# A two-layer decoder trunk: the residual rows keep their place in SBUF, the expert ring goes from 22 units to 20, and the router's place table is built by another chain

## The chip, the cores and the metric

One core of a Trainium2 chip runs the whole kernel. The metric is device time in microseconds, median of the runs. The engines are TensorE (PE in the profile, PEld for its weight loads), VectorE (DVE), ScalarE (ACT), GpSimd (POOL) and SyncE (SP). SP issues nearly all loads; in the profile "SPq" is a transfer issued from SP's queue.

## The reference, cut to what matters

Two layers run over 512 rows of width 1024 in f32. Layer 0 mixes by differential attention, layer 1 by latent attention. Each is followed by a mixture of experts with 32 experts, of which each row takes two:

```python
for i in range(DEPTH):                      # 2 layers
    h = modulate(rms_norm(x, norm_mix[i]), sh_m, sc_m)
    y = diff_attention(h, ...) if i % 2 == 0 else mla_attention(h, ...)
    x = x + g_m[:, None, :] * y
    h = modulate(rms_norm(x, norm_ffn[i]), sh_f, sc_f)
    x = x + g_f[:, None, :] * hier_moe(h, ...)   # top-1 of 4 groups, then top-2 of its 8 experts
...
hid = jax.nn.silu(t @ w1) * (t @ w3) * combine   # per expert, 1024 -> 256
out = out + hid @ w2                             # 256 -> 1024
```

The last addition of each layer needs x as it stood before the experts ran. These are the residual rows.

## The kernel before, in words

**Work.** The rows stand on chip in X, four tiles (t = 0 to 3) of 128 rows. After each attention comes a stage that adds the mixer's product to X (DVE L1931, L1932), normalises it into XN, writes XN to the DRAM tensor xn_d (POOL L2506), and computes the router's logits. The router (`gate` on DVE, `route` on PE) then picks two experts for each row and makes `idx`, the list of rows that each pair of experts gathers. Experts are worked on in 16 pairs (n = 0 to 15), 64 places for each expert. For a pair POOL gathers 128 rows of XN by indirect DMA into RV (L2515). PE turns them (L969 for the first pair, L951 for the others), ACT and DVE modulate them (DVE L2142, L2124), and PE multiplies by w1 (signals "a"), by w3 ("b") (both L979), turns the hidden rows (L986) and multiplies by w2 ("y", L994; L1009 for the last pair). DVE weighs the result (L2155), and POOL scatters it to y_d (L2529), except for the last pair, which PE adds by a product (L1084). What doesn't fit into 64 places goes through an extra tile ("overflow") between pairs 8 and 9. At the layer's end y_d is read back into Y, and DVE adds it to X.

**Weights.** Each pair needs six units of 1 MB: two of w1, two of w3, two of w2, so a layer needs 96. They go through a ring of places (SLOTS = 22). Three banks of six lie in the buffers ring, RQK and AHS, two places in the buffer spare, and two (slots 18 and 19, X_SLOT) are X itself. Unit u of a layer goes to `slot_order[l][u % SLOTS]`. SP issues the units in one fixed order: the first 18 or so while the attention stage runs, each once the buffer under it is free; then it waits for the first two gathers; then it loads the two X places, and from there on unit u waits for the product that last read unit u - SLOTS:

```python
if u < SLOTS:
    free_at_first(l, slot)
else:
    before, part = divmod(u - SLOTS, 6)
    sp.wait_ge(sem("aby"[part // 2]), PAIRS * l + before + 1)
```

**The rows meanwhile.** Since weights are laid over X, POOL writes X to kept_d after each tile's norm (L2507), and SP reads it back near the layer's end: for layer 0 in `stream(1)` (L501), for layer 1 after the last experts (L636). The SP program runs layer 0 and layer 1 one after the other; the layer 0 read of Y (L521, L525) waits for the last scatter, that of layer 1 is issued by ACT (L1676).

**Identity products.** `keep_busy(bank, n)` (L741) issues n products of the identity with itself, whose result nobody reads. The profile records two of them for each product.

Of the kernel before, what the change touches and what calls it, by code (L numbers as in the profile page):

```python
# [68 lines left out]
SLOTS = BANKS * RING + 4  # L69
END_BANKS = (2, 3), (4, 7), (0, 1), (5, 6)  # L70
X_SLOT = BANKS * RING
SPARE_AT = {22: X_SLOT + 2, 38: X_SLOT + 3}
# [157 lines left out]
def build(nc, A, out):  # L230
    stack = ExitStack()
    with stack:
# [16 lines left out]
        kept_d = [nc.dram_tensor(f"kept_d{l}", [S, D], F32) for l in range(2)]  # L249
# [151 lines left out]
        half_of, place, over_cap, raw = scratch(PS, 2 * T), scratch(PS, 2 * T), scratch(PS, 2 * T), scratch(PS, 2 * T)  # L401
# [36 lines left out]
        def unit(s):  # L438

            if s < RING:  # L440
                return ring[:, s, :]
            if s >= X_SLOT + 2:
                return spare[:, s - X_SLOT - 2]
            if s >= X_SLOT:
                return X[:, 2 * (s - X_SLOT):2 * (s - X_SLOT) + 2, :].rearrange("p t n -> p (t n)")
            base = RQK if s < 2 * RING else AHS
            return base[:, s % RING * UNIT:(s % RING + 1) * UNIT]
# [6 lines left out]
        plan, arrival, fills, holder = [], [{}, {}], [0] * SLOTS, [None] * X_SLOT  # L454
# [3 lines left out]
        fills[X_SLOT:] = [1, 1, 1, 1]  # L458
        for l in range(2):
# [10 lines left out]
            slot_order.append([14, 15] + list(range(RING, 2 * RING)) + [18, 19, 20, 21] + unheld + held + [16, 17, 12, 13])  # L470
# [4 lines left out]
            if l == 0:  # L475
                fills[X_SLOT:] = [n + 3 for n in fills[X_SLOT:]]
            holder = [("y", PAIRS - 2)] * RING + [None] * (2 * RING)
        in_x_slot = len([u for u in range(6 * PAIRS) if u % SLOTS == X_SLOT])
        for t in range(T):
            own = in_x_slot  # L480
            loaded["rows", t] = 16 * (1 + own + 2)
            loaded["mla", t] = loaded["rows", t] + 16
            loaded["last rows", t] = loaded["mla", t] + 16 * (own + (2 if t else 1))
        s_w = [sem(f"w{s}") for s in range(X_SLOT)] + [sem("xl0"), sem("xl1"), sem("xl2"), sem("xl3")]
# [13 lines left out]
        def _(sp):  # L498
# [12 lines left out]
            def stream(l):  # L511
                for n, entry in enumerate(plan[l]):
                    if l == 0 and n in SPARE_AT:
                        first_units(0, SPARE_AT[n])
                    if l == 1 and n == 0:
                        sp.wait_ge(sem("y"), LAST - 2)
                        load_x(kept_d[0], 0)
# [12 lines left out]
            def free_at_first(l, slot):  # L530
# [12 lines left out]
                elif slot < X_SLOT:  # L543
                    sp.wait_ge(*((sem("omla"), 8) if l else (sem("oe"), 8)))
                elif slot >= X_SLOT + 2:
                    if l:
                        sp.wait_ge(sem("res"), T + 1 + slot - X_SLOT)
                else:
                    sp.wait_ge(sem("kept_out"), 16 * T * (l + 1))
# [38 lines left out]
            for l in range(2):  # L588
# [14 lines left out]
                else:  # L603
                    first_units(1, 4, 5, 6, 7, 8, 9, 10, 11, 16, 17, 12, 13, 20, 0, 1, 2, 3, 21, 14, 15)
# [42 lines left out]
            sp.wait_ge(sem("out"), 16 * (T + 2))  # L647
# [3 lines left out]
        def _(pe):  # L651
# [266 lines left out]
            def route(l):  # L918

                pe.wait_ge(sem("el"), 2 * (l + 1))  # L920
                keep_busy(3, 16)
                pe.wait_ge(sem("M"), l + 1)
                ranks = PB[6][:, 0:T * E].rearrange("p (t e) -> p t e", t=T)
                mm(PB[6][:, 0:T * E], trib[:, :], Mb.rearrange("p t e -> p (t e)"), start=True, stop=False)
# [14 lines left out]
                keep_busy(3, 16 if l else 22)  # L939
# [785 lines left out]
        def _(dve):  # L1725
# [226 lines left out]
            def add_at_end():  # L1952

                dve.wait_ge(sem("out"), 16)
# [33 lines left out]
            def gate(l):  # L1988
# [46 lines left out]
                tt(hot_step, oh[:, :, 0:PAIRS], oh[:, :, PAIRS:], ALU.add)  # L2035
                link(red(half_of, oh[:, :, PAIRS:], AX.X, ALU.add))
# [597 lines left out]
```

## Time and profile before

| what | us |
|---|---|
| median of 3 runs | 1110.64 |
| lowest, highest | 1109.88, 1111.30 |
| the profiled execution, its time | 1109.18 |
| the profiled execution, its span in the trace | 1107.4 |
| mean granted clock of TensorE in it | 0.988 of full |

The trace covers the span of 1107.4 us; 1.8 us of the profiled execution's time lie around it. All positions in the text are microseconds from the span's start. The stage of layer 0's experts begins near 342, that of layer 1 near 856.

### The profile page before, as it was taken

The numbers are of one execution on the slowest core, as the hardware profiler recorded it, in microseconds if no ns is written. First come the engines' busy times: TensorE is split into PE (matmuls) and PEld (weight loads), VectorE is DVE, ScalarE is ACT, GpSimd is POOL, SyncE is SP. The second block draws the span as 40 slices with busy tenths as digits, with TensorE's granted clock in tenths as the row PEclk, the third lists the DMA queues.
The fourth block names the chain that finished last, engine by engine and source line by source line (L and its number), as shares of the span: only waits on it lengthen the run. The fifth ranks groups of instructions, "written<-read, shape, count | busy, mean of one in ns | idle before, by whom it ended". The sixth has DMA issues, their size and how long they took to land.

```text
span 1107.4 us, 15314 instructions
## 1 busy us (share of the span) xinstructions
PE 1041.3 (94%) x5662; PEld 630.0 (57%) x5662; DVE 611.5 (55%) x1479; ACT 328.6 (30%) x891; POOL 92.0 (8%) x129
## 2 busy tenths in 40 slices
PE   6999999999998999898889999999998899979986
PEld 5444444555458666565556566565456666646652
DVE  6799989898647422222246577877236622222224
ACT  4321111874231211111114555666122211111110
POOL 1000000000011212121000000000000111101100
PEclk8999999999998999999999999999999999999999
DMA  9939967947578999999996400401837899999998
GB/s 366 404 132 395 393 264 297 386 171 297 235 291 328 401 419 418 418 418 419 417 394 269 166 1 1 189 2 50 367 115 305 346 419 419 417 397 417 419 416 351
DMA packets 66814, 341.44 MB, mean 308 GB/s; under 512 B 11110, under 2 KB 11366, under 8 KB 36400
## 3 DMA queue, kind: packets, MB, share of 16 engines
q1 hardware_dynamic: 49952, 297.68, 66.7%
q0 software_dynamic: 15120, 37.63, 8.9%
q10 hardware_dynamic: 1664, 5.09, 1.2%
q8 instruction: 48, 0.79, 0.3%
q14 instruction: 30, 0.25, 0.1%
HBM read 320.90 MB, written 37.24 MB: 323 GB/s over the span
## 4 chain that ended last, share of the span: by engine, by line
PE 75%; DMA 10%; DVE 5%; SPq 4%; ACT 3%; issue 3%; ACTq 0%; DVEq 0%; POOLq 0%
PE PP L979 16%; PE PP L732 12%; PE PP L842 10%; PE PP L994 8%; DMA AHS<-in_moe_w 5%; SPq L565 4%; PE PP L754 3%; PE PP L1199 3%; PE PP L1165 2%; PE PP L1203 2%; DMA AHS<-y_d 2%; PE PP L802 2%; PE PP L705 2%; PE PP L791 2%; PE PP L951 1%
## 5 line engine op out<-in xcount | busy, mean ns | idle before, releaser
L732 PE MATMUL PP<-ring,AHS 128*128 128x512 f32 x320 | 139.9, 592 | 0.0
L2148 DVE TENSOR_TENSOR PS<-PS,PP 128x256 f32<-128x256 f32 x33 | 13.9, 421 | 193.2 <-PE PP L979 183.7
L842 PE MATMUL PP<-ring,AHS 128*128 128x512 f32 x256 | 112.2, 594 | 0.0
L732 PEld LDWEIGHTS PP<-ring,AHS 128*128 128x128 f32 x320 | 59.7, 190 | 69.8 <-issue 69.8
L2155 DVE SCALAR_TENSOR_TENSOR PS<-PP,small,GF 128x512 f32<-128x512 f32 x66 | 46.5, 747 | 95.8 <-PE PP L994 85.4
L842 PEld LDWEIGHTS PP<-ring,AHS 128*128 128x128 f32 x256 | 47.8, 190 | 56.9 <-issue 56.9
L1642 ACT ACTIVATE PS<-PP 128x256 f32<-128x256 f32 x33 | 12.6, 383 | 216.5 <-PE PP L979 186.8
L979 PE MATMUL PP<-RQK,RV 128*64 128x256 f32 x640 | 71.9, 379 | 2.7 <-issue 2.7
L979 PE MATMUL PP<-AHS,RV 128*64 128x256 f32 (+1 forms) x592 | 68.7, 380 | 2.3 <-DVE RV L2142 1.3
L979 PE MATMUL PP<-ring,RV 128*64 128x256 f32 (+1 forms) x528 | 64.3, 391 | 4.1 <-issue 2.1
L979 PEld LDWEIGHTS PP<-RQK,RV 128*64 128x64 f32 x640 | 54.7, 137 | 21.9 <-issue 8.9
L979 PEld LDWEIGHTS PP<-AHS,RV 128*64 128x64 f32 (+1 forms) x592 | 51.1, 138 | 19.5 <-issue 6.6
L979 PEld LDWEIGHTS PP<-ring,RV 128*64 128x64 f32 (+1 forms) x528 | 49.1, 144 | 20.7 <-issue 8.7
L2529 POOL DMA_INDIRECT y_d<-PS,row x31 | 31.8, 1027 | 329.0 <-DVE PS L2155 286.1
L1872 DVE TENSOR_REDUCE small<-PP 128x2 f32<-128x256 f32 (+3 forms) x64 | 52.5, 822 | 8.5 <-PE PP L757 8.4
L2124 DVE TENSOR_SCALAR RV<-PP,small 128x128 f32<-128x128 f32 x124 | 42.4, 406 | 24.1 <-PE PP L951 23.2
L1748 DVE SCALAR_TENSOR_TENSOR ring<-ring,PS 128x1024 f32<-128x1024 f32 x44 | 51.8, 1221 | 4.3 <-DMA ring<-in_ada_t 3.9
L1646 ACT ACTIVATE PS<-PP 128x256 f32<-128x256 f32 x33 | 12.6, 383 | 136.4 <-PE PP L986 136.4
L1618 ACT ACTIVATE RV<-PP,small 128x128 f32<-128x128 f32 x124 | 46.6, 456 | 3.5 <-PE PP L951 3.5
L741 PE MATMUL PP<-ident 128*128 128x128 f32 x280 | 40.3, 307 | 4.4 <-POOL GM L2435 2.2
L1429 ACT ACTIVATE AHS<-PP,small 128x256 f32<-128x256 f32 (+3 forms) x82 | 41.1, 510 | 11.0 <-DVE small L1872 10.8
L1748 DVE SCALAR_TENSOR_TENSOR AHS<-AHS,PS 128x1024 f32<-128x1024 f32 x36 | 42.5, 1222 | 1.5 <-DMA AHS<-in_ada_t 1.0
(366 smaller groups left out, 1711.4 us busy)
## 6 DMA issues: line engine op xcount, KB each, us to landing
AHS<-in_moe_w SPq DMA_DIRECT2D x54, 1024.0 KB, 23.0
RQK<-in_moe_w SPq DMA_DIRECT2D x52, 1024.0 KB
ring<-in_moe_w SPq DMA_DIRECT2D x49, 1024.0 KB, 21.9
ring<-in_ada_t SPq DMA_DIRECT2D x22, 1024.0 KB, 21.1
AHS<-in_ada_t SPq DMA_DIRECT2D x18, 1024.0 KB
spare<-in_moe_w SPq DMA_DIRECT2D x16, 1024.0 KB, 13.6
X<-in_moe_w SPq DMA_DIRECT2D x16, 1024.0 KB
ring<-in_da_w_qkv SPq DMA_DIRECT2D x10, 1024.0 KB, 13.3
```

What stands on the lines that cost most here:

```text
L565: sp.dma_start(unit(slot), (w1, w3, w2)[k // 2][l][n + PAIRS * (k % 2)]).then_inc(s_w[slot], 16)
L732: last = mm(PB[qkv_bank(n)][:, :], HT[:, c, t * P:(t + 1) * P], us[c // 4][:, (c % 4) * NH:(c % 4 + 1) * NH], start=c == 0, stop=c == C - 1)
L741: mm(PB[bank][:, 0:P], ident[:, :], ident[:, :], start=True, stop=True)
L842: last = mm(PB[2 * t + n][:, :], (OT, OTM)[l][:, k, t * P:(t + 1) * P], us[k // 2][:, (k % 2) * D + n * NH:(k % 2) * D + (n + 1) * NH], st ...
L979: last = mm(o[s0:s1, 0:FF], xgT[b][:, c, s0:s1], w(2 * m + e)[:, c * FF:(c + 1) * FF], start=c == 0, stop=c == C - 1)
L994: last = mm(PB[5 + m][s0:s1, :], hidT[:, c, s0:s1], w(4 + e)[:, c * D + m * NH:c * D + (m + 1) * NH], start=c == 0, stop=c == 1)
L1429: last = fn(dst, src, ACT.Exp, bias=nmx[:, b, a:a + 1], accum_out=total)
L1618: last = fn(xgT[b][:, c, :], PB[0][:, (c // 2) * P:(c // 2 + 1) * P], ACT.Identity, bias=MODC[:, l, 3 + V_SHIFT, c:c + 1], scale=GC[:, 2 * ...
L1748: last = stt(wt, wt, 1.0, condb, ALU.mult, ALU.mult, accum_out=MODC[:, l, w, 2 * q + c:2 * q + c + 1])
L1872: red(nmx[:, b], o, AX.X, ALU.max, negate=True).then_inc(sem("nm"), 1)
L2124: last = ts(xgT[b][:, c, :], PB[1][:, (c // 2) * P:(c // 2 + 1) * P], GC[:, 2 * l + 1, c:c + 1], MODC[:, l, 3 + V_SHIFT, c:c + 1], ALU.mul ...
L2155: last = stt(ysb[b][:, cols], PB[5 + m][:, :], weight, GF[:, cols], ALU.mult, ALU.mult)
```

## The change

The change has two independent parts.

**Rows and ring.** kept_d is gone: neither the eight writes of X nor the eight reads back are issued, and X is no place for weights. SLOTS becomes 20 (18 plus the two spare places, now numbered 18 and 19). The order of places is turned so that the first pair uses ring places and AHS, and the units that SP loads right after the first two gathers are now units 20 to 23, which wait for the products of pair 0. DVE no longer waits at the end for the reread tile 0.

**Router.** Before, a row's place was the rank in its expert, plus 64 if the expert is in the upper half, plus 1024 if the rank is 64 or more, and two comparisons of 512 columns built the one-hot table. Now PE adds 8 x 128 = 1024 to the ranks of the upper experts by one more product, a second table of column numbers (`iota_h`, upper half from 1024 on) is compared with the rank, and eight comparisons of 128 columns in f16 build the table. The copy of the ranks comes after `idx` and takes the 1024 off again. In layer 0 the identity products behind `idx` are 16 instead of 22.

```diff
-SLOTS = BANKS * RING + 4
+HALF = 1024
+SLOTS = BANKS * RING + 2
...
-            slot_order.append([14, 15] + list(range(RING, 2 * RING)) + [18, 19, 20, 21] + unheld + held + [16, 17, 12, 13])
+            slot_order.append(held[2:] + held[:2] + [16, 17, 12, 13, 14, 15] + list(range(RING, 2 * RING)) +
+                              list(range(SPARE_SLOT, SLOTS)) + unheld)
...
                     if l == 1 and n == 0:
-                        sp.wait_ge(sem("y"), LAST - 2)
-                        load_x(kept_d[0], 0)
                         sp.wait_ge(sem("rows"), 1)
...
                         for t in (1,) if n == 2 else (2, 3):
-                            load_x(kept_d[0], t)
                             sp.dma_start(Y[t], y_rows[0][t]).then_inc(sem(f"xl{t}"), 16)
...
                 for b in range(2):
                     sp.wait_ge(sem(f"gath{b}"), 16 * (PAIRS // 2 * l + 1))
-                first_units(l, 18, 19)
-                experts(l, BANKS, (4, 5))
+                experts(l, BANKS, (2, 3, 4, 5))
...
-            sp.wait_ge(sem("y"), PAIRS + LAST - 2)
-            for t in range(T):
-                sp.dma_start(X[:, t, :], kept_d[1][t * P:(t + 1) * P, :]).then_inc(sem(f"xl{t}" if t else "out"), 16)
...
                 pe.wait_ge(sem("el"), 2 * (l + 1))
                 keep_busy(3, 16)
+                pe.wait_ge(sem("iota"), 2 * l + 1)
+                ranks = PB[6][:, 0:T * E].rearrange("p (t e) -> p t e", t=T)
+                mm(ranks, onesb[:, :], eights.unsqueeze(1).broadcast_to([P, T, E]), start=True, stop=False)
                 pe.wait_ge(sem("M"), l + 1)
-                mm(PB[6][:, 0:T * E], trib[:, :], Mb.rearrange("p t e -> p (t e)"), start=True, stop=False)
+                mm(PB[6][:, 0:T * E], trib[:, :], Mb.rearrange("p t e -> p (t e)"), start=False, stop=False)
...
                 pe.wait_ge(sem("idx"), 2 * l + 1)
-                keep_busy(3, 16 if l else 22)
+                keep_busy(3, 16)
...
             def add_at_end():
 
-                dve.wait_ge(sem("out"), 16)
                 dve.wait_ge(sem("mix"), T + 1)
...
-                tt(hot_step, oh[:, :, 0:PAIRS], oh[:, :, PAIRS:], ALU.add)
-                link(red(half_of, oh[:, :, PAIRS:], AX.X, ALU.add))
+                link(tt(hot_step, oh[:, :, 0:PAIRS], oh[:, :, PAIRS:], ALU.add))
                 tt(hot_token, hot_step, over(token_v.rearrange("p t k -> p (t k)"), 2, PAIRS), ALU.mult)
-                link(ts(half_of, half_of, float(CAP), None, ALU.mult))
                 dve.wait_ge(sem("rank"), 2 * l + 1)
                 link(tt(picked, OH, over(PB[6][:, 0:T * E].rearrange("p (t e) -> p t e", t=T), 2, 2), ALU.mult))
                 link(red(raw, slots, AX.X, ALU.add))
-                ts(over_cap, raw, CAP - 0.5, 1024.0, ALU.is_ge, ALU.mult)
-                link(tt(place, raw, half_of, ALU.add))
-                link(tt(place, place, over_cap, ALU.add))
-                for h in range(2):
-                    js = slice(T * h, T * h + T)
-                    tt(hot_place[:, js], over(place[:, js], 2, P), over(iota_p, 1, T), ALU.is_equal).then_inc(sem("hotp"), 1)
+                for j in range(2 * T):
+                    last = ts(hot_place[:, j], iota_h, raw[:, j:j + 1], None, ALU.is_equal)
+                    if j % T == T - 1:
+                        last.then_inc(sem("hotp"), 1)
                 dve.wait_ge(sem("rank"), 2 * l + 2)
                 link(v.tensor_copy(cnt, PB[7][:, T * E:(T + 1) * E]))
-                v.tensor_copy(rank, PB[6][:, 0:T * E].rearrange("p (t e) -> p t e", t=T))
                 dve.wait_ge(sem("tab"), 2 * l + 1)
                 ts(idx[:, 0:PAIRS], PB[2][:, 0:PAIRS], -1.0, float(S), ALU.mult, ALU.add).then_inc(sem("idx"), 1)
+                stt(rank, over(eights, 1, T), -float(P), PB[6][:, 0:T * E].rearrange("p (t e) -> p t e", t=T), ALU.mult, ALU.add)
...
+                    g.iota(iota_h.rearrange("p (a b c d) -> p a b c d", a=2, b=2, c=8), [[HALF, 2], [32, 2], [1, 8], [8, 4]],
+                           base=0, channel_multiplier=0, allow_small_or_imprecise_dtypes=True)
+                    g.iota(eights, [[HALF // P, 2], [0, PAIRS]], base=0, channel_multiplier=0, allow_small_or_imprecise_dtypes=True)
...
                     pool.dma_start(xn_d[l][t * P:(t + 1) * P, :], XN[:, t, :]).then_inc(sem("xd"), 16)
-                    pool.dma_start(kept_d[l][t * P:(t + 1) * P, :], X[:, t, :]).then_inc(sem("kept_out"), 16)
```

## Rows read from the trace of the kernel before

**Rows 1.** The profile's page: the span in 40 slices, bytes moved in each.

```profile
GB/s 366 404 132 395 393 264 297 386 171 297 235 291 328 401 419 418 418 418 419 417 394 269 166 1 1 189 2 50 367 115 305 346 419 419 417 397 417 419 416 351
```

**Rows 2.** Busy time by windows: PE, PEld, DVE, ACT, POOL, clock, DMA share, GB/s.

```profile
345.00:350.00 5.00, 4.72 (x36) 4.48 (x35) 2.29 (x7) 0.68 (x2) 0.38 (x1) 0.85 0.56 139
380.00:400.00 20.00, 19.28 (x146) 12.46 (x144) 4.99 (x12) 4.43 (x12) 4.60 (x5) 1.00 1.01 417
990.00:994.00 4.00, 2.00 (x5) 0.57 (x3) 1.47 (x3) 0.00 (x0) 0.00 (x0) 1.00 0.79 283
```

**Rows 3.** The chain that ended last, in order of time: start, us, what.

```profile
360.77 3.65 PE PP L994 x16
...
372.96 3.65 PE PP L994 x16
...
517.65 29.84 DMA AHS<-in_moe_w
...
1039.68 29.54 DMA AHS<-in_moe_w
...
1083.96 17.46 DMA AHS<-y_d
```

**Rows 4.** Timeline of SP: start, us, what was issued.

```profile
348.28 0.80 SPq L565 DMA_DIRECT2D X<-in_moe_w  x2
354.09 1.95 SPq L565 DMA_DIRECT2D AHS<-in_moe_w  x2
...
862.92 0.80 SPq L565 DMA_DIRECT2D X<-in_moe_w  x2
866.65 0.81 SPq L565 DMA_DIRECT2D AHS<-in_moe_w  x2
```

**Rows 5.** Timeline of PE: start, us, what, count, idle before it.

```profile
342.04 6.80 PE L741 MATMUL PP<-ident 128*128 128x128 f32 x44 [0.27 <-DVE idx L2052]
348.69 1.04 PE L969 MATMUL PP<-ident,RV 128*128 128x128 f32 x8
...
855.87 3.84 PE L741 MATMUL PP<-ident 128*128 128x128 f32 x32 [0.27 <-DVE idx L2052]
861.19 1.09 PE L969 MATMUL PP<-ident,RV 128*128 128x128 f32 x8 [1.49 <-DMA RV<-xn_d,idx]
873.48 3.65 PE L994 MATMUL PP<-RQK,PS 128*64 128x512 f32 x16 [0.38 <-ACT PS L1646]
1085.07 1.94 PE L1009 MATMUL PP<-RQK,PS 128*64 128x512 f32 x8 [0.28 <-DMA RQK<-in_moe_w]
```

**Rows 6.** Timeline of DVE in layer 1's router and the tile after it.

```profile
852.20 0.29 DVE L2037 TENSOR_TENSOR PS<-PS 128x128 f16<-128x128 f32 x1
...
852.61 0.42 DVE L2040 TENSOR_TENSOR PS<-PS,PP 128x256 f32<-128x256 f32 x1
...
853.52 0.17 DVE L2042 TENSOR_SCALAR PS<-PS 128x8 f32<-128x8 f32 x1
...
853.99 1.29 DVE L2047 TENSOR_TENSOR PS<-PS 128x512 f16<-128x512 f32 x2
...
862.06 1.37 DVE L2142 TENSOR_SCALAR RV<-PP,small 128x128 f32<-128x128 f32 x4 [1.37 <-PE PP L969]
```

**Rows 7.** DVE operations whose scalar is read from memory: one by lines, one pair by timeline.

```profile
L2318 DVE TENSOR_SCALAR PS<-PS,small 128x128 f32<-128x128 f32 x14 | 3.4, 283 | 0.2
...
L2266 DVE TENSOR_SCALAR AHS<-PP,small 128x128 f32<-128x128 f32 x8 | 2.4, 346 | 0.1
```

```profile
601.65 0.61 DVE L2266 TENSOR_SCALAR AHS<-PP,small 128x128 f32<-128x128 f32 x2
```

**Rows 8.** Timeline of DVE: the first add of layer 1, and the end.

```profile
567.92 2.48 DVE L1980 TENSOR_TENSOR X<-X,AHS 128x1024 f32<-128x1024 f32 x2 [0.24 <-DMA AHS<-y_d]
...
1101.44 1.22 DVE L1967 TENSOR_TENSOR X<-X,AHS 128x1024 f32<-128x1024 f32 x1 [0.24 <-DMA AHS<-y_d]
1103.56 1.29 DVE L1971 TENSOR_TENSOR X<-X,PP 128x512 f32<-128x512 f32 x2 [0.89 <-PE PP L1098]
```

More of the change, by code:

```diff
@@ L68 @@
 BANKS = 3
-SLOTS = BANKS * RING + 4
+HALF = 1024
+SLOTS = BANKS * RING + 2
 END_BANKS = (2, 3), (4, 7), (0, 1), (5, 6)
-X_SLOT = BANKS * RING
-SPARE_AT = {22: X_SLOT + 2, 38: X_SLOT + 3}
+SPARE_SLOT = BANKS * RING
+SPARE_AT = {22: SPARE_SLOT, 38: SPARE_SLOT + 1}
 ADA_SLOTS = (4, 5, 12, 13)
@@ L248, in build @@
         x_d = nc.dram_tensor("x_d", [S, D], F32)
-        kept_d = [nc.dram_tensor(f"kept_d{l}", [S, D], F32) for l in range(2)]
         y_d = [nc.dram_tensor(f"y_d{l}", [2 * S, D], F32) for l in range(2)]
@@ L400, in build @@
         hot_step, hot_token = scratch(PS, 2 * T, PAIRS), scratch(PS, 2 * T, PAIRS, dt=F16)
-        half_of, place, over_cap, raw = scratch(PS, 2 * T), scratch(PS, 2 * T), scratch(PS, 2 * T), scratch(PS, 2 * T)
+        raw, iota_h, eights = scratch(PS, 2 * T), scratch(PS, P, dt=F16), scratch(PS, E, dt=BF16)
         assert at[0] <= 2816
@@ L441, in unit @@
                 return ring[:, s, :]
[L442 to L445, printed above, removed]
+            if s >= SPARE_SLOT:
+                return spare[:, s - SPARE_SLOT]
             base = RQK if s < 2 * RING else AHS
@@ L453, in build @@
         streams = ring_plan(A)
-        plan, arrival, fills, holder = [], [{}, {}], [0] * SLOTS, [None] * X_SLOT
+        plan, arrival, fills, holder = [], [{}, {}], [0] * SLOTS, [None] * SPARE_SLOT
         holder[RING + 4] = ("dat", 16)
@@ L457, in build @@
         loaded = {}
-        fills[X_SLOT:] = [1, 1, 1, 1]
+        fills[SPARE_SLOT:] = [1, 1]
         for l in range(2):
@@ L475, in build @@
             if l == 0:
-                fills[X_SLOT:] = [n + 3 for n in fills[X_SLOT:]]
+                fills[SPARE_SLOT:] = [n + 2 for n in fills[SPARE_SLOT:]]
             holder = [("y", PAIRS - 2)] * RING + [None] * (2 * RING)
-        in_x_slot = len([u for u in range(6 * PAIRS) if u % SLOTS == X_SLOT])
+        in_spare = [len([u for u in range(6 * PAIRS) if slot_order[0][u % SLOTS] == s]) for s in range(SPARE_SLOT, SLOTS)]
         for t in range(T):
-            own = in_x_slot
-            loaded["rows", t] = 16 * (1 + own + 2)
+            own = in_spare[t - 2] if t >= 2 else 0
+            loaded["rows", t] = 16 * (1 + own + 1)
             loaded["mla", t] = loaded["rows", t] + 16
-            loaded["last rows", t] = loaded["mla", t] + 16 * (own + (2 if t else 1))
-        s_w = [sem(f"w{s}") for s in range(X_SLOT)] + [sem("xl0"), sem("xl1"), sem("xl2"), sem("xl3")]
+            loaded["last rows", t] = loaded["mla", t] + 16 * (own + 1)
+        s_w = [sem(f"w{s}") for s in range(SPARE_SLOT)] + [sem("xl2"), sem("xl3")]
         w1 = [A["moe_w1"][l].rearrange("g e (p c) f -> (g e) p (c f)", c=C) for l in range(2)]
@@ L542, in free_at_first @@
                     sp.wait_ge(sem("lg"), 4 * (l + 1))
-                elif slot < X_SLOT:
+                elif slot < SPARE_SLOT:
                     sp.wait_ge(*((sem("omla"), 8) if l else (sem("oe"), 8)))
[L545 to L549, printed above, removed]
+                elif l:
+                    sp.wait_ge(sem("res"), T + 3 + slot - SPARE_SLOT)
             def first_units(l, *slots):
@@ L646, in _ @@
                         sp.dma_start(out[rows, cols], X[:, t, cols]).then_inc(sem("out"), 16)
-            sp.wait_ge(sem("out"), 16 * (T + 2))
+            sp.wait_ge(sem("out"), 16 * (T + 1))
         @block.tensor
```

3 lines of the change are left out of this document (1 added, 2 removed).

## Prediction

> **What bounds the kernel now.** I read the page's slices first. The line of bytes moved shows two long plateaus at 417 to 420 GB/s, slices 14 to 20 and 33 to 40 [rows 1]. These are the two expert stages. Nothing in the trace moves more than these 0.42 MB/us over a long stretch, so I take the plateau as the most that the transfers give. The windows say the same with a second column: from 380 to 400 the DMA engines are busy all the time (share 1.01) while PE is busy too [rows 2]. Both are full, and the question is which ends last.
>
> The chain that ended last answers it. In both layers it leaves PE near the end of the stage and runs through a load of expert weights that took 29.5 to 29.8 us from issue to landing [rows 3]. One unit is 1.05 MB, which at 0.417 MB/us is 2.5 us. A landing time of 30 us means twelve units in the queue: the load isn't late because it was issued late, it stands behind other loads. So the end of each expert stage is set by bytes: by the moment from which the transfers run without a break, plus all that has to go through them. From one pair's "y" product to the next PE took 12.2 us (360.77 to 372.96) [rows 3]. The transfers need 15 for the six units and about 1.2 for a gather and a scatter, each some 64 rows of 4 KB (1024 chosen places over 16 pairs): about 16. PE lives on its stock of units, and what counts is how many lie on chip when the unbroken run begins.
>
> When does it begin? Between 345 and 350 the share is 0.56 at 139 GB/s [rows 2]: SP has loaded 20 units and has nothing more that it may issue. It resumes at 348.28 with the two units for X, and at 354.09 with the next two, when pair 0's first product is done. In layer 1 the same two moments are 862.92 and 866.65 [rows 4].
>
> **Part 1, the ring of 20.** The two X units go; they were the 21st and 22nd. Units 20 and 21 now wait for pair 0's first product ("a" of pair 0). So 76 units remain in either case, but their run starts later. The shift depends on how far part 2 pulls "a" forward, so that comes first.
>
> **Part 2, the router.** In layer 1, between 852.20 and `idx`, DVE does the following [rows 6].
> (a) L2036 and L2038 go. Only L2037 is still ahead of L2040, which could then start at 852.20 instead of 852.61: 0.4 us in layer 1. In layer 0 the two also go, but there the rank products end just as DVE is ready for them, and the additional product on PE comes in front. I take 0.
> (b) L2042 to L2044 go, which stand between 853.52 and 853.99: 0.47 us in each layer.
> (c) Two comparisons of 512 columns took 1.29 us together. Eight of 128 columns take their place, each with its scalar read from memory. No row shows such a thing in f16. The nearest is an f32 operation of that shape and kind at 283 ns. Two like it in a row, source in PSUM, took 0.61 us at 0.346 each, so they overlap by 0.08 and one starts 0.26 after the other [rows 7]. With 283 ns and the same overlap the distance is 0.20, and eight take 7 x 0.20 + 0.28 = 1.68 us, which is 0.39 more than before. Bounds: at the PSUM distance 7 x 0.26 + 0.35 = 2.17 (0.88 more); if only the 0.08 between the starts of tiny operations counted, about 0.8 (0.5 less). I take +0.39.
> The Trainium skill ("VectorE: DVE Perf Modes", Mode 4x_2P) says that a one-source operation with 16-bit data on both sides in SBUF handles four elements in a cycle, against two for f32. No row here shows it; by it, as an estimate from the page's clock, each comparison would be some 0.03 us shorter than the f32 row, and all eight would cost 0.1 more than before instead of 0.39.
> (d) The copy of the ranks moves behind `idx`. `idx` waited for PE's table in any case, so nothing is gained. Behind it DVE is idle before it modulates the first pair, 1.37 us in layer 1 [rows 6], and takes the 0.3 there. The new product is under 0.25 us; two more fills on POOL lie in 14 us of its idle time. Both at 0.
>
> `idx` comes 0.47 - 0.39 = 0.1 us earlier in layer 0 and 0.4 + 0.1 = 0.5 us in layer 1.
>
> From `idx` to the first turn of rows, the layers differ [rows 5]. In layer 1 PE is through with 16 identity products at 859.7 and waits 1.49 us for the gather until 861.19. The gather is what counts, and it moves by 0.5. In layer 0, 22 products (44 records, 6.80 us) end at 348.8 and the turn follows at once. The gather had landed before: in layer 1 it came 5.3 us after PE saw `idx` (855.87 to 861.19), and the same from 342.04 is 347.4. Layer 1's products show 0.12 us per record at full clock; twelve records fewer are 1.44 us. (The group in layer 0 averages 0.155 because the clock was at half in its middle; the records that go are the last ones, at full clock.) The turn moves to about 347.2, and the gather, 0.1 earlier too, is there by 347.3; I let the 0.1 go. "a" of pair 0 gains 1.5 us in layer 0 and 0.5 in layer 1. All that PE does until it starves moves along.
>
> **Back to part 1, layer 0.** Before: two units from 348.28, done 5.0 us later at 353.3, a gap of 0.8, then the run from 354.09 on with 74 units. After: "a" at 352.6, with 76 units. The two extra cost 5.0, the earlier start gives back 1.5: **+3.5 us**.
>
> **Layer 1.** Before, the two units from 862.92 last until 867.9, beyond 866.65, so the run is unbroken from 862.92. After, it begins at 866.65 - 0.5 = 866.15: +3.2. The four units of "a" and "b" then last 10 us, until 876.15, and the next ones wait for "y" of pair 0, which comes at 873.48 + 3.65 [rows 5], less 0.5, = 876.6: a new gap of 0.5. Against it, before has a hole that fills: around the overflow tile SP may issue nothing until that tile is done, and the transfers ran dry, 283 GB/s on average from 990 to 994 [rows 2]. Against 419 that is 1.3 us of full rate missing. With the transfers 3.7 us behind and PE 0.5 ahead, their queue is not empty there. Sum 3.2 + 0.5 - 1.3 = **+2.4 us**.
>
> **What kept_d gives back.** Writes: sixteen transfers of 0.52 MB go, 8.4 MB in all, or 20 us of transfer time. The eight writes fall in stretches that end in idle transfers before the experts (139 GB/s at 345), or between stages. They only lengthen that idleness: 0. If that cover were gone, each layer's four would be worth 5.0 us. Reads of layer 0: tile 0 stands in the queue between the last weights and Y. Y landed 0.24 us after DVE was ready [rows 8], so of the 1.25 us that tile 0 took, 0.2 count: **-0.2 us**; afterwards PE works without a gap and the other three tiles are covered. Reads of layer 1: they stand in SP's queue behind the last weights (1085.07 [rows 5]), beside the Y loads that ACT issues. The chain's last load takes 17.46 us [rows 3]; without 2.1 MB beside it the last Y lands 5.0 us earlier. But then DVE's own work is next: it waited 0.24 us for Y and 0.89 for the product of the last tile [rows 8], the earlier adds follow PE. So **-1.1 us** and not 5.
>
> **Sum.** 3.5 - 0.2 + 2.4 - 1.1 = +4.6 us. Against the profiled execution's time, 1109.18 (its span 1107.4 and 1.8 around it), that is 1113.8. The median of the runs is 1.46 above that execution, so the same sum gives 1115.2.
>
> Bounds: the comparisons at their fast bound move "a" 0.9 further forward, at their slow one 0.5 back. So layer 0 lies between +2.6 and +4.0, and layer 1 between +1.0 (fast, no new gap, the hole filled) and +4.2 (slow, the gap, the hole as before). End and transition lie between -1.3 and 0. Together +2.3 to +8.2, or 1112.9 to 1118.8.
>
> **The rivals.**
> *A, the stock is not missed (faster).* If the last weights would land in time with two units fewer in stock, only the gains are left: 1.5 + 0.5 + 0.2 + 1.1 = 3.3 us, 1107.3. It decides where the last loads have 5.0 us of slack in layer 0 and 3.7 in layer 1. For it: PE is 96% busy from 380 to 400 [rows 2]. Against it: PE waits for weights at 1085.07, and 30 us of queue in both layers. Chance 0.10.
> *B, one layer swallows it (no change).* In layer 1 PE is the slower side up to the overflow tile, as the hole in the transfers shows. If the refilled queue makes up for all of the late start there, layer 1 gives -0.5 instead of +2.4: +1.7 us in all, 1112.3. Against it: the hole measures only 1.3 us. Chance 0.14.
> *C, the volume counts (much faster).* By the whole kernel's share of busy transfers, 8.4 MB fewer are 20 us, minus the 5.9 that the ring costs: about 1096. Against it: the writes fall where transfers pause. Chance 0.02.
> *D, the clock (slower).* PE starves earlier in the stage. If TensorE's clock fell to 1.2 GHz for the last pair, its last product alone, two halves of 1.94 us at full clock [rows 5], would cost 3.9 us more, the products before it as much again or more: 1119 and up. For it: the clock does fall in a pause, 0.85 of full from 345 to 350 [rows 2]. Against it: the kernel fills the pause before the last pair with identity products, and at the transfers' pace that pause is as long as before. Chance 0.08.
> The forecast keeps 0.66.
>
> **Numbers.** Forecast 1115.2. Two in a thousand, 2.2 us, is about what a measurement of this kernel tells from no change. Slower: the forecast's whole mass but 0.04, plus D: 0.70. Same: most of B, the low end of the forecast: 0.17. Faster: A, C and a little of B: 0.13. The range goes from 1109.0, below B, to 1118.8, the upper bound; outside lie A, C and most of D. The likeliest case alone spans 1112.9 to 1118.8.
>
> **What would show it.** In SP's timeline no load between the gathers and "a" of pair 0; that "a" at 352.6 and, layer 1's own delay taken off, 0.5 earlier; nearly no transfers from 345 to 352. The first add of Y of layer 0 (567.92 before [rows 8]) at 571.2, the last half of L1009 in layer 1 (1085.07 before) at 1090.8. No dip in GB/s at the overflow tile. The last Y landing well before DVE needs it. If instead L1009 stays where it was, the stock was never the limit and A holds; if `idx` is later than before, the eight comparisons were mis-sized; if the end gains 5 us, DVE was not next.

## The result, and the profile after

The changed kernel takes 1115.04 us (median of 13 runs, 1112.06 to 1118.23); the kernel before, on the same chip, 1109.88 (13 runs, 1107.47 to 1111.88). The ratio is 1.0055, with a 95% interval of 1.0044 to 1.0065: 6.1 us slower by the ratio, 5.2 by the medians. The profiled execution of after is the slowest of its 13, 1118.23, with a span of 1116.5. Against the 1107.4 of before that is 9.1 us, so some 3 us of what the two traces show belong to these two executions and not to the change. The experiments tell which.

What transfers did around pair 0 and at the overflow tile, in the windows of after (columns as in [rows 2]):

```profile
340.00:345.00 5.00, 3.84 (x37) 3.46 (x37) 4.40 (x25) 0.00 (x0) 1.03 (x1) 1.00 0.31 128
345.00:350.00 5.00, 2.84 (x24) 2.41 (x22) 3.38 (x14) 0.84 (x3) 1.09 (x2) 1.00 0.46 118
350.00:355.00 5.00, 4.77 (x45) 3.86 (x47) 4.55 (x19) 2.34 (x4) 0.99 (x1) 1.00 0.22 48
355.00:360.00 5.00, 5.00 (x47) 4.27 (x43) 2.69 (x8) 0.00 (x0) 0.00 (x0) 1.00 0.93 367
...
985.00:990.00 5.00, 4.99 (x23) 4.43 (x24) 0.00 (x0) 0.00 (x0) 0.35 (x1) 1.00 1.00 411
990.00:995.00 5.00, 3.53 (x14) 2.23 (x14) 0.42 (x1) 0.97 (x3) 0.00 (x0) 1.00 1.02 422
995.00:1000.00 5.00, 2.81 (x9) 1.03 (x8) 1.47 (x3) 0.00 (x0) 0.00 (x0) 1.00 1.02 423
```

The same stretch in before:

```profile
350.00:355.00 5.00, 4.62 (x44) 3.73 (x46) 4.55 (x20) 2.49 (x5) 0.99 (x1) 1.00 0.97 408
```

From 350 to 355 the transfers move 48 GB/s, where before they moved 408: with a ring of 20 nothing may be issued until "a" of pair 0 is done. The hole at the overflow tile, 283 GB/s in [rows 2], is gone (422 and 423).

SP's and PE's timelines of after, layer 0 and then layer 1 (they answer to [rows 4] and [rows 5]):

```profile
353.99 4.20 SPq L558 DMA_DIRECT2D ring<-in_moe_w  x4
...
874.20 4.20 SPq L558 DMA_DIRECT2D ring<-in_moe_w  x4
```

```profile
333.42 6.29 PE L730 MATMUL PP<-ident 128*128 128x128 f32 x32 [0.59 <-DVE PS L1990]
339.55 0.22 PE L913 MATMUL PP<-PS,onesb 128*128 128x128 bf16 x1
...
342.91 3.84 PE L730 MATMUL PP<-ident 128*128 128x128 f32 x32 [0.34 <-DVE idx L2037]
348.47 1.09 PE L960 MATMUL PP<-ident,RV 128*128 128x128 f32 x8 [1.72 <-DMA RV<-xn_d,idx]
...
568.53 1.94 PE L1000 MATMUL PP<-RQK,PS 128*64 128x512 f32 x8 [0.82 <-DMA RQK<-in_moe_w]
...
851.73 6.54 PE L730 MATMUL PP<-ident 128*128 128x128 f32 x32 [0.66 <-DVE PS L1990]
858.11 0.22 PE L913 MATMUL PP<-PS,onesb 128*128 128x128 bf16 x1
...
867.63 1.97 PE L960 MATMUL PP<-ident,RV 128*128 128x128 f32 x8 [2.33 <-DMA RV<-xn_d,idx]
```

The first L730 group of each layer (L741 before) are the 16 identity products that `route` issues ahead of the ranks. Their 32 records took 5.25 us in layer 0 of before and 3.84, at full clock, in layer 1; here 6.29 and 6.54. The windows say why for layer 1: a granted clock of 0.50, which is 1.2 GHz, under after's products, and 1.00 under the same products before.

```profile
852.00:857.00 5.00, 5.00 (x24) 5.00 (x25) 4.34 (x26) 0.00 (x0) 0.00 (x0) 0.50 1.03 424
```

```profile
847.20:851.00 3.80, 3.80 (x32) 3.64 (x32) 3.29 (x23) 0.20 (x1) 0.00 (x0) 1.00 1.02 419
```

(After's window first, then before's.) The ranks (L913 and on) stand behind them and came late. In layer 0 the turn of rows then waits for the gather: "a" is done at 353.99, 0.1 earlier than before instead of 1.5.

In DVE's timeline of after (layer 1's comparisons, first add of Y, the end; compare [rows 6] and [rows 8]):

```profile
859.42 1.39 DVE L2031 TENSOR_SCALAR PS<-PS 128x128 f16<-128x128 f16 x8
...
572.45 2.48 DVE L1970 TENSOR_TENSOR X<-X,AHS 128x1024 f32<-128x1024 f32 x2 [0.46 <-DMA AHS<-y_d]
...
1107.70 1.29 DVE L1961 TENSOR_TENSOR X<-X,PP 128x512 f32<-128x512 f32 x2 [1.80 <-PE PP L1089]
```

And in the chain that ended last, of after:

```profile
502.10 32.65 DMA ring<-in_moe_w
...
559.70 7.88 DMA y_d<-PS,row
567.63 4.79 DMA AHS<-y_d
...
862.24 5.35 DMA RV<-xn_d,idx
...
1034.11 29.18 DMA ring<-in_moe_w
```

Both layers still go through some 30 us of queued expert weights (32.65 and 29.18); only the load of Y at the very end, 17.46 us in [rows 3], has left the chain.

The two traces, cut at the same events (us). "Start" is PE's first identity product ahead of the ranks, "a" SP's first issue behind pair 0's "a", T the second half of the last output product (L1009, L1000 after):

| stretch | before | after | difference |
|---|---|---|---|
| span start to layer 0's start | 333.28 | 333.42 | +0.1 |
| start to "a", layer 0 | 20.81 | 20.57 | -0.2 |
| "a" to T, layer 0 | 210.13 | 214.54 | +4.4 |
| T to layer 1's start | 282.97 | 283.20 | +0.2 |
| start to "a", layer 1 | 19.46 | 22.47 | +3.0 |
| "a" to T, layer 1 | 218.42 | 221.10 | +2.7 |
| T to the end | 22.33 | 21.20 | -1.1 |

The +3.0 is the odd one, and it has three parts: the ranks come 1.8 us later behind the slower identity products, the rows 0.8 later from the gather, and the turn of rows and "a" take 1.1 more (the turn alone 1.97 us instead of 1.09); against that the router's own chain is 0.7 shorter. Where both halves of the last output product stand in one group of a timeline, as in layer 1 of after, T is the group's end less the 1.94 us of a half (here 1095.30).

### The profile page after: what moved, and what is told of

The parts are those of the page before. It is cut to its first block, busy times and chain, and to the rows that moved or that the text cites. A ratio compares the mean times of both kernels' runs of the same rounds, so it can differ in the third digit from the quotient of the medians.

```text
span 1116.5 us, 15283 instructions
## 1 busy us (share of the span) xinstructions
PE 1044.8 (94%) x5652; PEld 632.0 (57%) x5652; DVE 610.1 (55%) x1481; ACT 329.1 (29%) x891; POOL 88.7 (8%) x125
## 3 DMA queue, kind: packets, MB, share of 16 engines
q10 hardware_dynamic: 1664, 5.09, 1.2%
## 4 chain that ended last, share of the span: by engine, by line
PE 73%; DMA 10%; DVE 7%; issue 4%; ACT 4%; SPq 1%; DVEq 0%; ACTq 0%; POOLq 0%
PE PP L970 18%; PE PP L721 10%; PE PP L831 10%; PE PP L985 9%; DMA ring<-in_moe_w 6%; DMA ring<-in_ada_t 3%; PE PP L743 3%; PE PP L1190 3%; PE PP L1156 2%; PE PP L1194 2%; PE PP L791 2%; PE PP L780 2%; PE PP L730 2%; PE PP L942 1%; PE PP L1206 1%
## 5 line engine op out<-in xcount | busy, mean ns | idle before, releaser
L970 PE MATMUL PP<-ring,RV 128*64 128x256 f32 (+1 forms) x672 | 79.7, 382 | 8.6 <-issue 5.8
L970 PE MATMUL PP<-RQK,RV 128*64 128x256 f32 x640 | 76.4, 397 | 10.2 <-issue 8.0
L970 PE MATMUL PP<-AHS,RV 128*64 128x256 f32 x640 | 73.6, 386 | 3.9 <-issue 3.9
L970 PEld LDWEIGHTS PP<-ring,RV 128*64 128x64 f32 (+1 forms) x672 | 60.3, 140 | 29.4 <-issue 15.3
L970 PEld LDWEIGHTS PP<-AHS,RV 128*64 128x64 f32 x640 | 54.9, 139 | 23.4 <-issue 10.4
L2517 POOL DMA_INDIRECT y_d<-PS,row x31 | 31.7, 1024 | 338.9 <-DVE PS L2141 288.9
L730 PE MATMUL PP<-ident 128*128 128x128 f32 x268 | 41.8, 324 | 4.2 <-POOL GM L2421 2.2
L730 PEld LDWEIGHTS PP<-ident 128*128 128x128 f32 x268 | 39.8, 236 | 7.6 <-issue 2.9
```

The lines of the kernel that those rows point to most:

```text
L730: mm(PB[bank][:, 0:P], ident[:, :], ident[:, :], start=True, stop=True)
L970: last = mm(o[s0:s1, 0:FF], xgT[b][:, c, s0:s1], w(2 * m + e)[:, c * FF:(c + 1) * FF], start=c == 0, stop=c == C - 1)
```

## The experiments

Eleven kernels, each with a profile and timed against before; "+" is us over before, from the ratio times before's median, with its 95% interval. The runs were made in three sessions, e1 to e4, e5 to e7 and e8 to e11, each on another chip and each beside runs of before; figures are compared across sessions only by way of before. First come the two parts by themselves, then two doses.

**e1, the ring alone.** Ring of 20 and rows kept on chip; router and 22 products of before.

```diff
-                keep_busy(3, 16)
+                keep_busy(3, 16 if l else 22)
...
-                for j in range(2 * T):
-                    last = ts(hot_place[:, j], iota_h, raw[:, j:j + 1], None, ALU.is_equal)
+                for h in range(2):
+                    js = slice(T * h, T * h + T)
+                    tt(hot_place[:, js], over(place[:, js], 2, P), over(iota_p, 1, T), ALU.is_equal)...
```

> The change's ring of 20 and the rows kept on chip, with the router of before and its 22 identity products in layer 0. Theory (the run of expert loads starts later, the stock is what is missed): +5.0 us in layer 0 for two units, +2.9 in layer 1 (the start 3.7 later, less 1.3 for the hole at the overflow tile, with the 0.5 gap), -0.2 and -1.1 at the ends: 6.6 us over before. Rival 1 (the new router and its weaker cover of the clock are what costs): about 3 us over before, since in the profile of after the router's part was 0.9 and 3.5 us longer. Rival 2 (the stock is not missed): -1.3 us.

Measured: 1.0052, +5.8 us (3.8 to 7.8). The ring alone gives the loss of the whole change; neither the 3 us of the first rival nor a gain fits.

**e2, the router alone.** The ring of 22, its X places and `kept_d` of before; router and 16 products of after (`SLOTS = BANKS * RING + 4`).

> The change's router and its 16 identity products in layer 0, with the ring of 22 and the rows written out and read back as before. Theory (each part by itself as predicted, the clock as in the profile of before): at most -0.9 in layer 0 (the two units for X's place start the run, only the gap of 0.8 behind them closes) and -0.5 in layer 1: -0.5 to -1.4 us. Rival 1 (the router is what costs): +1.5 to +3 us. If neither sign shows, the identity products saved are lost again in waiting for the gather.

Measured: 1.0002, +0.2 us (-1.4 to +1.9). The theory's gain of 0.5 to 1.4 us lies in the interval, and so does no gain at all; of the rival's loss of 1.5 to 3 us only the lowest part does. Its profile has what the last sentence names, a turn of rows in layer 0 that waits for the gather:

```profile
343.35 3.84 PE L742 MATMUL PP<-ident 128*128 128x128 f32 x32 [0.34 <-DVE idx L2050]
348.53 1.09 PE L972 MATMUL PP<-ident,RV 128*128 128x128 f32 x8 [1.35 <-DMA RV<-xn_d,idx]
```

**e3, a ring of 18.** After, without the two places in `spare`: `SLOTS = BANKS * RING`, `SPARE_AT = {}`. The order in which units take their places is turned as well, so that the first pair fits into 18. (The expectation speaks of X's places; they took no unit in after already, and the two that go are those in `spare`.)

> The changed kernel with a ring of 18: X's places take no unit at all, so two units fewer are in stock, and nothing else changes. Theory: two more units move behind the first product in each layer, 5.0 us of transfers each; some 10 us over after in all, about 16 over before. In layer 1 up to 2.5 us may be covered by PE being the slower side before the overflow tile. Rival (one layer swallows it): 5 us over after. Rival (the stock is not missed): 0.

Measured: 1.0133, +14.8 us (12.1 to 17.5), so 8.7 over after, near the theory's 10; 5 lies outside what the two intervals allow, and 0 far outside. The trace gives the dose without the clock's scatter. In layer 0 "a" is at 352.72 and T at 572.21, 219.49 apart; in layer 1 877.49 and 1103.73, 226.24. Against after that is 4.95 and 5.1 more: two units are 5 us of transfers in each layer, and neither swallows any. Something else is in it that no one expected: from T of layer 0 to layer 1's start e3 takes 284.96 us, where the twelve other kernels take 282.6 to 283.2. These 1.8 to 2.3 us were not followed up. The total hides them, since from start to "a" e3 is 1.2 and 2.15 us shorter than after, in layer 0 and 1.

**e4, a ring of 20, rows out and back.** e1 plus `kept_d`: the same stock, 8.4 MB more.

```diff
+            for t in range(T):
+                sp.dma_start(X[:, t, :], kept_d[1][t * P:(t + 1) * P, :])...
...
+                    pool.dma_start(kept_d[l][t * P:(t + 1) * P, :], X[:, t, :])...
```

> As the first kernel of this call (ring of 20, router of before), but X is written out and read back as before, though its places in the ring stay free. It has the same stock and 8.4 MB more traffic. Theory (the writes fall where transfers pause, of the reads 0.2 us are on the path in layer 0 and 1.1 at the end): 1.3 us over the first kernel. Rival (the volume counts): 20 us over it. Rival (the reads at the end cost all of their transfer time): 6 us over it.

Measured: 1.0064, +7.1 us (5.1 to 9.1), 1.3 over e1. The intervals overlap, so the times alone don't show it; the traces do, and put it in one place. From T to the end e4 takes 22.45 us (1091.05 to 1113.5), e1 21.16 (1093.24 to 1114.4). Twice at the end of e4 DVE waits for Y again, 0.41 and 0.37 us; the second time with the last tile:

```profile
1107.55 1.23 DVE L1965 TENSOR_TENSOR X<-X,AHS 128x1024 f32<-128x1024 f32 x1 [0.37 <-DMA AHS<-y_d]
1109.66 1.28 DVE L1969 TENSOR_TENSOR X<-X,PP 128x512 f32<-128x512 f32 x2 [0.89 <-PE PP L1096]
```

Of the 20 us that 8.4 MB take, written and read back, nothing more shows than the 1.3 us that the theory gave. Both rivals, 20 us and 6 us over e1, are out.

**e5, e6, e7, fewer identity products ahead of the ranks.** 6 instead of 16, in before (e5), in after (e6) and in e2 (e7).

```diff
                 pe.wait_ge(sem("el"), 2 * (l + 1))
-                keep_busy(3, 16)
+                keep_busy(3, 6)
```

> The kernel before with 6 identity products ahead of the rank products in place of 16, in both layers. They only keep TensorE's clock up. At full clock 16 take 3.84 us and end before the chosen experts are known; at the lower level 6.3 to 6.5 us, and the ranks wait. Theory: where the clock is low at that point, the ranks come 1.2 to 1.7 us earlier per layer, where it is full nothing changes: 0 to -3 us, about -1 on average. Rival (fewer products let the clock fall for the ranks, the table and the first pair): +1 to +3 us.

> The changed kernel with 6 identity products ahead of the ranks in place of 16, in both layers. Theory (in the profile of after they took 6.3 and 6.5 us and held up the ranks): -1 to -3 us against after. Rival (the clock falls instead for what follows): +1 to +3 us against after. Third: nothing, if the profile of after was an odd execution in this and the median has them at full clock.

> The second kernel of this study (new router, ring of 22, rows out and back) with 6 identity products ahead of the ranks: the version that would beat both kernels if the router's own gain and the fewer products add up. Theory: -1 to -3 us against before. Rival (the clock falls for the first pair): 0 to +3 us.

Measured: e5 1.0015, +1.7 us (0.6 to 2.8); e6 1.0030, +3.3 (2.2 to 4.5), 2.8 under after, as its theory had it; e7 1.0003, +0.3 (-1.0 to +1.7). The ranks did stop waiting for PE in all three, and with the new router the turn of rows came 13.3 to 13.8 us after the start, against 13.8 to 15.9 in after and e2. In e5, with the old router, it came no earlier: 15.4 and 15.0, against 15.4 and 14.0 in before, as in layer 1 the products behind `idx` now ran at the low clock (6.47 us for 3.84). So e7 should have won. Its trace shows why it didn't, and it is nothing that any expectation named. Here are the timelines behind the overflow tile of layer 1: PE in before, then PE and DVE in e7:

```profile
994.27 5.36 PE L979 MATMUL PP<-spare,RV 128*64 128x256 f32 x32 [2.27 <-DVE PS L2155]
```

```profile
986.97 3.70 PE L997 MATMUL PP<-AHS,PS 128*128 128x512 f32 x8 [0.47 <-ACT PS L1649]
...
990.71 1.41 DVE L2154 SCALAR_TENSOR_TENSOR PS<-PP,small,GF 128x512 f32<-128x512 f32 x2 [4.71 <-PE PP L997]
...
999.04 2.40 PE L982 MATMUL PP<-spare,RV 128*64 128x256 f32 x10 [8.37 <-issue]
```

PE stands still for 8.37 us where 2.27 were enough in before; all that it waits for by the profile ended at 992.12 ("issue" is idle time with no releaser). At this place the program jumps over the code of the overflow tiles that aren't taken. In e7 the last loads have landed before PE asks, and the last product runs without a wait (1085.82, 3.65 us for both halves). So PE is the bound of layer 1: its second half starts at 1087.53, where the transfers, 218.2 us behind "a" as in before, would have allowed 1083.5. Part of that comes back, since the last loads are then early: from T to the end e7 takes 21.17 us, before 22.33. In e6 the same stall, 7.76, costs nothing, since with a ring of 20 the transfers are the slower side to the end (its second half at 1089.93 waits for weights).

The four kernels below test what the stall hangs on: 20 identity products put back at the very start, now only 8 columns wide, in e7 (e8), e5 (e9) and e6 (e10); and before with 20 taken out at its start, nothing else (e11).

```diff
             keep_busy(7, 14)
+            for _ in range(20):
+                mm(PB[7][:, 0:8], ident[:, :], ident[:, 0:8], start=True, stop=True)
```

```diff
-                keep_busy(0, 8)
...
-            keep_busy(7, 14)
+            keep_busy(7, 2)
```

> The new router, the ring of 22 and 6 identity products ahead of the ranks, as in an earlier kernel of this study, plus 20 identity products of 8 columns at the kernel's very start, where PE waits 3.85 us anyway. In the three kernels with 6 products PE stood still for 7.8 to 8.4 us behind the overflow tile of layer 1, against 2.1 to 2.3 in the six others, and no wait explains it. The only thing that they share is that 20 products fewer lie in PE's instruction stream ahead of that tile. Theory (the place of the jump in the stream decides): with the 20 put back the stall is 2.2 us again, PE is no longer behind the transfers in layer 1, and the kernel takes 1.5 to 3 us less than before. Rival (something in the router's own timing causes the stall): 8.4 us again and no gain over the kernel without the 20.

> The kernel before with 6 identity products ahead of the ranks and the same 20 thin ones at the start. Theory (place in the stream): the stall behind the overflow tile is 2.2 us, and the time is that of before or up to 1 us over it, since the second group of 22 and 16 products then runs at the lower clock, 6.8 and 6.5 us. Rival: 8.4 us of stall and 1.7 us over before, as without the 20.

> The changed kernel with 6 identity products ahead of the ranks and the same 20 thin ones at the start. In the ring of 20 the transfers are the slower side up to the end and swallowed the stall. Theory: 2.2 us of stall in place of 7.8, and no change of the time, 3 us over before or up to 1 less. Rival: if the time falls by the 5.6 us of the stall, PE was the bound there after all.

> The kernel before with 20 identity products taken out at its very start (12 of 14 and all 8 of the next group), nothing else. Theory (place in the stream): PE stands still for about 8.4 us behind the overflow tile of layer 1, 860 us later, and the kernel takes 2 to 4 us more than before, up to 1 us of it at the start from TensorE's lower clock. Rival (the stall belongs to the router's timing): 2.2 us of stall as before, and 0 to 1 us more.

Measured: e8 0.9989, -1.2 us (-2.6 to +0.1); e9 1.0001, +0.1 (-1.1 to +1.2); e10 1.0032, +3.5 (2.3 to 4.7); e11 1.0035, +3.9 (2.2 to 5.7). The same place in e8's and in e11's timeline of PE:

```profile
992.64 5.36 PE L982 MATMUL PP<-spare,RV 128*64 128x256 f32 x32 [2.11 <-DVE PS L2156]
```

```profile
1000.90 2.40 PE L978 MATMUL PP<-spare,RV 128*64 128x256 f32 x10 [8.35 <-issue]
```

The stall goes with 20 products put back 980 us earlier (2.11, 2.10 and 2.19 us in e8, e9, e10), and comes in a kernel whose router was never touched. So it doesn't belong to the router; it hangs on how many of PE's instructions lie ahead of the jump.

The traces also show what arrives while PE stands. The queue q8 carries instructions: 48 packets of 16 KB in each of the thirteen traces. Its share, and that of q14, which carries instructions too, in three windows: in e8 from 970.0 to 992.6, where PE goes on; in e7 from 970.0 to 990.7, where PE stops; in e7 from there to 999.0, where it goes on.

```profile
q8 instruction: 1, 0.02, 0.3%
q14 instruction: 1, 0.01, 0.1%
```

```profile
q14 instruction: 1, 0.01, 0.1%
```

```profile
q8 instruction: 1, 0.02, 0.7%
```

More finely, e8's packet starts at 979.8, during the overflow tile, 12.8 us before PE goes on. In e7 none comes in that tile; the packet starts at 996.4, when PE has stood for 5.7 us, and PE goes on 2.6 us after it. It is the same in all thirteen: in the nine without the stall a packet starts 11.2 to 13.1 us before PE goes on, in the four with it 2.6 to 2.8 us before. So in the stall PE very likely waits for a block of its own instructions. That q8 is PE's queue, and that this packet holds the code behind the jump, is read from the timing and not shown.

Of e11's 3.9 us about 1 lies at the start (layer 0's start 334.32 against 333.28). e10 is no faster than e6, which shows again that a ring of 20 leaves PE slack. e9, at +0.1, also speaks for the stall as what e5 lost by: by the ratios it is 1.6 us, though the two intervals just touch.

e8 is the fastest of the thirteen kernels, 1.2 us under before, where 1.5 to 3 were expected. Its interval just reaches zero, so it is a likely gain and not a shown one; it is under the 0.2% that a measurement tells from no change.

e8 and e9, made on one chip, differ only in the router and in 16 or 22 products behind `idx` in layer 0, and so do e7 and e5. Layer 1 of e9, then of e8:

```profile
848.30 2.34 PE L741 MATMUL PP<-ident 128*128 128x128 f32 x12 [0.82 <-DVE PS L2002]
...
856.99 6.51 PE L741 MATMUL PP<-ident 128*128 128x128 f32 x32 [0.27 <-DVE idx L2054]
```

```profile
846.47 2.32 PE L742 MATMUL PP<-ident 128*128 128x128 f32 x12 [0.82 <-DVE PS L2005]
...
854.55 3.84 PE L742 MATMUL PP<-ident 128*128 128x128 f32 x32 [0.34 <-DVE idx L2052]
```

From the start to the products behind `idx` it is 8.69 us in e9 and 8.08 in e8. By the ratios the new router is worth 1.3 us in either pair. Each pair by itself is hardly beyond the noise, since each of the four intervals reaches 1.1 to 1.3 us to either side; the two together, with the traces, make a gain likely. So the router does give something back where PE's 16 products no longer stand ahead of it.

## Why the prediction was right, point by point

The forecast was 1115.2 and the median is 1115.04. That they are so close is luck. The forecast was 4.6 us over before and the measured difference is 6.1 by the ratio; that the medians hide this comes in part from the base, which was 1110.64 in the 3 runs that the prediction had and is 1109.88 in 13. The direction, the cause and the size of the main term held; the smaller half of the sum did not. The ring was to cost 6.6 us (the sum without the router's 2.0) and costs 5.8 in e1 (3.8 to 7.8). The router was to give back 2.0 in a ring of 20, and after lies 0.3 over e1, where the two intervals together leave about 2.3 us to either side: nothing shows, and the full 2.0 is at the edge of what fits. (e2, with its ring of 22, is no test of the 2.0; there 0.5 to 1.4 were expected.) So a gain that was put too high was offset by a ring that cost 0.8 less than forecast and a base that lay 0.8 lower. Of the signs named ahead, the first add of Y in layer 0 came at 572.45 (571.2 forecast) and the last half of layer 1 at 1095.30 (1090.8 forecast). Both are late by about what "a" is late by in that layer of this trace, 1.4 us in layer 0 and 4.7 in layer 1.

**Part 1, layer 0 ("the two extra cost 5.0").** Measured by "a" to T. With 18 it is 219.49. With 20 it is 214.54, 214.65, 214.47, 214.69 and 214.55 (after, e1, e4, e6, e10). With 22 it is less sharp, since there the transfers start with the two X units and not with "a": 210.13, 209.63, 210.32 and 209.58 (before, e5, e9, e11), where "a" comes 5.8 to 6.6 us behind the X units, and 210.29, 210.82 and 211.13 (e2, e7, e8), where it comes within their 5.0 us and the transfers have no gap. So 18 to 20 is 5.0 as costed, and 20 to 22 is 4.2 to 5.1 where before's gap exists; against before itself it is 4.4. The missing 0.6 was not followed up. (The prediction's reading of the plateau, "slices 14 to 20 and 33 to 40" at 417 to 420, is a little too wide: slices 14, 36 and 40 stand at 401, 397 and 351 in [rows 1]. Nothing in the sum hangs on it.)

**Part 1, layer 1 ("3.2 later, 0.5 gap, -1.3 for the hole").** From "a" that is 3.7 + 0.5 - 1.3 = 2.9. With 22: 218.42, 218.08, 218.27 and 218.13 (before, e2, e8, e9); with 20: 221.10, 221.22, 221.20, 221.14 and 221.22 (after, e1, e4, e6, e10). The difference is 2.7 to 3.1, as forecast. Left out are e5, e7 and e11, whose stall makes PE the bound (220.6 to 222.4). Rival B (one layer swallows it) falls with that and with e3.

**`kept_d`.** The end: -1.1 predicted, 22.33 to 21.20 measured, with e1, e6 at 21.16, 21.17 and e4 back at 22.45. "DVE's own work is next" held: from 1107.70 on DVE works to the end without a wait in after. The transition: -0.2 predicted; -0.3 in e1, e6 and e10 (282.63, 282.63, 282.65 against 282.97), +0.2 in after. Rival C is dead with e4.

**Part 2, `idx`.** Step (c) was mis-sized: the eight comparisons took 1.39 us, not 1.68. By the Trainium skill's rule ("VectorE: DVE Perf Modes", Mode 4x_2P) the prediction had estimated 0.1 more than the 1.29 us of the two wide ones, and the trace agrees. So the router's own chain is better than costed. Where the ranks wait for DVE and not for PE, from rank products to the identity products behind `idx` it takes 3.34 us (861.80 to 865.14 in e3) against 4.05 (851.82 to 855.87 in before): 0.7 less where 0.5 was forecast. Where PE comes late, 3.36, with the new product in it, against 3.67: 0.3 where 0.1 was forecast. With only 6 products ahead of the ranks, the way from the start to the products behind `idx` is 8.69 us in both layers of e5 and e9 and 7.99 to 8.09 in both layers of e6, e7, e8 and e10. There `idx` comes 0.6 to 0.7 us earlier in either layer.

**Part 2, the way to "a" ("the turn moves to about 347.2").** This is the step that failed. The prediction moved "a" of layer 0 by what happens from DVE's chain on (0.1 for `idx`, 1.4 for the six products) and put the 16 identity products ahead of the ranks at nothing, without a word. They were hidden only where they took 3.84 us, since the chosen experts are known 4.6 us after the start (847.19 to 851.82 in before); at 5.2 to 6.8 us they are on the path. In layer 0, from before to after, the ranks came 1.0 us later (5.09 and 6.13 us after the start), the router's chain was 0.3 shorter, the way from `idx` to the turn 1.1 shorter, and the rest 0.1 longer. Together that is 0.2 and not 1.5. e3 bears this out: there the 16 products took 5.31 us, much as in before (5.25), and the turn came at 347.20 and "a" at 352.72, where the prediction had 347.2 and 352.6. In the seven kernels with 16 of them the ranks came 4.6 to 6.6 us after the start. That is a scatter of up to 2 us a layer, and it makes 1.8 of the 3.0 us in layer 1 of the two profiles.

The 1.4 us for the six products hung on the clock too. Before's 22 products took 6.80 us at a clock that was low in their middle. From PE's start behind `idx` to the turn of rows, in layer 0 of all thirteen:

| kernel (products) | their time | to the turn | ended by |
|---|---|---|---|
| before (22) | 6.80 | 6.65 | PE |
| e5 (22) | 6.84 | 6.69 | PE |
| e11 (22) | 6.81 | 6.65 | PE |
| e9 (22) | 7.56 | 7.40 | PE |
| e1 (22) | 5.18 | 5.32 | both |
| e4 (22) | 5.18 | 5.36 | gather |
| after (16) | 3.84 | 5.56 | gather |
| e2 (16) | 3.84 | 5.18 | gather |
| e3 (16) | 3.84 | 5.35 | gather |
| e6 (16) | 4.25 | 5.32 | gather |
| e7 (16) | 5.61 | 5.72 | both |
| e8 (16) | 5.75 | 5.59 | PE |
| e10 (16) | 5.77 | 5.60 | PE |

At full clock 22 products already end with the gather, and taking six away is worth next to nothing (e1 and e4). At the low clock, which four of the six kernels with 22 show, it is worth 0.9 us and more. Each kernel has one trace, so whether the low clock belongs to the execution or to the kernel isn't shown. The gather isn't fixed at the 5.3 us of the prediction either: where it is what ends the wait, the turn comes 5.0 to 6.2 us behind PE's start (the 6.2 in layer 1 of after).

**Rivals A and D.** A is dead: two units missing from the stock cost 5.0 us in each layer from 20 to 18, and 4.4 and 2.7 from before to after. D (the clock at the last pair) did not occur: the last product's halves took 1.94 each in after.

## What to carry to other kernels

A place in a prefetch ring is worth its transfer time in each stage whose start is bound by stock, and traffic that falls where transfers pause is worth next to nothing; trade the one for the other only in that knowledge. Here two 1 MB places were worth 3 to 5 us in each layer and 8.4 MB of traffic 1.3 us. Cut traces at the events between which one resource sets the pace ("a" to T here): such stretches repeated within 0.2 us over the five kernels with a ring of 20, while their spans lay 5.7 us apart. Where something else starts that resource, as the X units do in layer 0 with a ring of 22, the same stretch spreads over 1.6 us. Filler products that keep the clock up must be priced at the low clock, where they are longest and stand in front of what they were meant to help; a term that is hidden in one trace still needs its price. And before reading anything from a small edit to an engine's stream, look at the idle time behind each jump in both traces.

## What the runs showed of the hardware that was not expected

**A jump can cost 6 us by how much lies ahead of it.** Behind the overflow tile of layer 1 PE is idle for 2.1 to 2.3 us in nine of the thirteen traces (before, after, e1 to e4, e8 to e10), and for 7.76 to 8.41 us with no releaser in e5, e6, e7 and e11, all of them with 20 products fewer ahead of it than their nearest relative without the stall. Twenty products are enough to switch it on and off. The Trainium skill ("Runtime: NRT & Kernel Launch", Instruction fetch mechanics) says that engines stream their instructions in blocks, and that a taken jump to a block that isn't there has to fetch it first. The traces agree as far as they go: a packet of the instruction queue q8 starts in each of the four stalls, 2.6 to 2.8 us before PE goes on, and in the nine other kernels it starts 11.2 to 13.1 us before. The number of packets, 48, is the same in all thirteen; only their time differs. Layer 0 has a stall of this kind in every kernel, before and after too: at its jump PE is idle for 2.9 to 4.0 us with no releaser, and goes on 2.3 to 2.8 us after a packet. In layer 1 the stall adds about 6 us of idle time whenever it occurs, and whether it costs anything depends on which side is the slower: by the ratios 1.6 us between e5 and e9 and 1.5 between e7 and e8, nothing between e6 and e10.

**The clock of a stretch differs between traces of the same operations.** The same 16 identity products behind the same wait took 3.84 to 6.76 us over seven kernels, at a granted clock between 2.4 and 1.2 GHz. In layer 0, where the six kernels before, after and e1 to e4 have the same operations on PE up to that point, they took 5.25, 6.29, 6.26, 6.76, 5.31 and 3.84 us. With 6 products instead the low stretch did not vanish. In e5 it moved to the ten records behind the ranks (2.48 in place of 1.36 us) and, in layer 1, to the second group (6.47 us, 3.84 in before).
